# Attention of a hybrid decoder layer: head pairs packed in 32 rows and row halves, mask as bias rows, transposes moved among the projection's products

## The reference

```python
h = rmsnorm(x, g_pre1) * (1 + scale1) + shift1           # shift, scale, gate from silu(c) @ w_ada
q, k, v, f, u, bg, cg, ga, gb = split(h @ w_in)
logf = log_sigmoid(f + b_f); cum = cumsum(logf)
# prompt: 256 queries, causal.  sample: 256 cached keys (2 pages) and 4 new ones per sequence
logit[t, s] = q_t . k_s / 8 + cum[t] - cum[s]            # s <= t, else -inf
o = softmax(logit) @ v
y = bg * conv3_causal(cg * u)
m = (sigmoid(ga) * (o @ w_oa) + sigmoid(gb) * (y @ w_ob)) @ w_o
x = x + gate1 * rmsnorm(m, g_post1)
x = x + gate2 * rmsnorm(swiglu(rmsnorm(x, g_pre2) * (1 + scale2) + shift2), g_post2)
```

## Time and profile before

| | us |
|---|---|
| median of 3 runs | 1874.73 (1874.23 to 1874.82) |
| profiled execution, its own time | 1877.05 |
| its span | 1875.4 |
| TensorE busy | 1831.7 |
| DVE busy | 901.9 |
| ACT busy | 730.7 |
| POOL busy | 52.5 |

### The profile page before, as it was taken

One profiled execution on the slowest core, in us unless ns is written; L12 is line 12 of the kernel. 1 busy time (PEld: TensorE's weight loads), 2 busy tenths in 40 slices (PEclk: granted clock), 3 DMA queues, 4 the chain that ended last, 5 costly groups with the idle time before them and its releaser, 6 DMA issues.

```text
span 1875.4 us, 33218 instructions
## 1 busy us (share of the span) xinstructions
PE 1831.7 (98%) x13960; PEld 1701.7 (91%) x13960; DVE 901.9 (48%) x1102; ACT 730.7 (39%) x886; POOL 52.5 (3%) x109
## 2 busy tenths in 40 slices
PE   8999999998889999999999999999999999999997
PEld 5889988885569999999978999999999999999996
DVE  4456653326753444445457343443444445565565
ACT  3433233325653433334346333333333334445453
POOL 0001000004200000000000000000000000000000
PEclk9999999999989999999999999999999999999999
DMA  9996968874454554547875574455445445445441
GB/s 347 386 322 226 330 226 315 314 257 152 164 171 160 170 165 157 168 167 269 291 280 178 193 247 158 157 162 173 157 162 172 158 160 174 159 159 175 161 158 51
DMA packets 189562, 382.17 MB, mean 204 GB/s; under 512 B 8773, under 2 KB 9245, under 8 KB 189183
## 3 DMA queue, kind: packets, MB, share of 16 engines
q1 hardware_dynamic: 185744, 378.04, 58.3%
q0 software_dynamic: 1312, 2.58, 0.4%
q10 hardware_dynamic: 2424, 0.37, 0.1%
HBM read 376.15 MB, written 4.81 MB: 203 GB/s over the span
## 4 chain that ended last, share of the span: by engine, by line
PE 93%; DVE 2%; ACT 2%; issue 1%; DMA 1%; POOL 0%; ACTq 0%; DVEq 0%; POOLq 0%
PE bank L553 28%; PE bank L555 27%; PE bank L554 27%; PE bank L563 4%; PE bank L872 1%; PE bank L587 1%; PE bank L806 1%; PE bank L789 1%; DMA ada<-in_w_ada 1%; PE bank L571 1%; PE bank L820 0%; PE bank L824 0%; PE bank L615 0%; ACT w_hi L996 0%; DVE w_lo L1407 0%
## 5 line engine op out<-in xcount | busy, mean ns | idle before, releaser
L553 PE MATMUL bank<-a_lo,w_hi 128*128 128x288 f32 x3648 | 1084.2, 297 | 5.1 <-DVE a_lo L1555 3.2
L554 PE MATMUL bank<-a_hi,w_hi 128*128 128x288 f32 x3648 | 1076.2, 295 | 0.0
L555 PE MATMUL bank<-a_hi,w_lo 128*128 128x288 f32 x3648 | 1072.8, 294 | 0.0
L1407 DVE TENSOR_TENSOR w_lo<-raw,w_hi 128x2048 fp32r<-128x2048 f32 x244 | 559.3, 2292 | 740.3 <-ACT w_hi L996 739.5
L996 ACT CAST w_hi<-raw 128x2048 fp32r<-128x2048 f32 x244 | 465.6, 1908 | 828.0 <-PE bank L555 828.0
L553 PEld LDWEIGHTS bank<-a_lo,w_hi 128*128 128x128 f32 x3648 | 683.7, 187 | 23.7 <-issue 17.3
L555 PEld LDWEIGHTS bank<-a_hi,w_lo 128*128 128x128 f32 x3648 | 687.1, 188 | 0.0
L554 PEld LDWEIGHTS bank<-a_hi,w_hi 128*128 128x128 f32 x3648 | 685.0, 188 | 0.0
L1519 DVE TENSOR_TENSOR a_lo<-hid,a_hi 128x1152 fp32r<-128x1152 f32 x44 | 59.4, 1352 | 12.3 <-ACT a_hi L1026 12.3
L563 PE MATMUL bank<-ada,cT 128*32 128x512 f32 x544 | 63.1, 596 | 1.7 <-DMA ada<-in_w_ada 1.7
L1026 ACT CAST a_hi<-hid 128x1152 fp32r<-128x1152 f32 x44 | 50.7, 1155 | 0.0
(11 more groups left out here) (306 smaller groups left out, 1068.9 us busy)
## 6 DMA issues: line engine op xcount, KB each, us to landing
raw<-in_w_ffn_in SPq DMA_DIRECT2D x88, 1024.0 KB, 5.0
raw<-in_w_in SPq DMA_DIRECT2D x80, 1024.0 KB, 6.5
ada<-in_w_ada SPq DMA_DIRECT2D x68, 1024.0 KB, 9.1
raw<-in_w_ffn_out SPq DMA_DIRECT2D x44, 1024.0 KB, 5.1
ada_o<-in_w_ada SPq DMA_DIRECT2D x26, 1024.0 KB, 9.6
raw<-in_w_o SPq DMA_DIRECT2D x16, 1024.0 KB, 5.6
raw<-in_cache_k SPq DMA_DIRECT2D x16, 512.0 KB, 4.7
raw<-in_cache_v SPq DMA_DIRECT2D x16, 512.0 KB, 4.5
```

The lines of the kernel that those rows point to most:

```text
L553: pe.matmul(acc, w_hi[buf][:, a, cols], lo[:, kt, :], start=first and a == 0, stop=False)
L554: pe.matmul(acc, w_hi[buf][:, a, cols], hi[:, kt, :], start=False, stop=False)
L555: mm = pe.matmul(acc, w_lo[buf][:, a, cols], hi[:, kt, :], start=False, stop=last and a == SK - 1)
L1407: tt(w_lo[buf][:, :, :], raw[s][:, :, :], w_hi[buf][:, :, :].bitcast(F32), ALU.subtract).then_inc(raw_turn, 1)
```

## The change

1. **Sampled sequences.** Two head pairs share the 32 rows of a column tile (8 rows each, `q_bd` 80 wide), so that all 16 heads lie in one bank: one pass of bias rows and two passes of q by K, and P by V with 256 columns. The mask is in the bias rows (`cumk`, `selq`, prepared once by POOL); ACT takes the exponential straight from the bank.
2. **Prompt.** q is scaled when it is copied to `qT`, and `qT`, `kT` and v rows are used in place. The two heads of a pair lie on partitions 0 to 63 and 64 to 127 and are multiplied as two row tiles into banks 0 and 1; -cum (`ncum`) is added by a matmul with K = 16. The row term cum[t] is dropped, since it cancels in the softmax. P by V of the pair is issued head by head in column halves. `extra_rows`, `copy_k`, `copy_q`, `v_st` are gone.
3. **Order.** The q, k, v stage is written out: w_ada groups after products 0, 2, 5, 7, 10, 12, 15, 17; z, lf, the sums, the suffix sums, k rows, v rows 0 to 1 of the first half and the first sequence's K pages among the products. Turns 1 to 7 start with `sample_scores`. The first mix product has the last sequence's P by V inside it, `keep_warm` is gone, and the split of y follows mix product 4.

The core of the diff:

```diff
-    ADA_EVERY = 3
+    ADA_AT = (0, 2, 5, 7, 10, 12, 15, 17)
...
-                for hf in range(2):
-                    for q4 in range(4):
-                        acc = bank[6 + hf][32 * q4:32 * q4 + 32, 0:PAST + TS]
-                        pe.matmul(acc, q_bd[:, 4 * hf + q4, :], KTs[j][:, 4 * hf + q4, :], start=True, stop=False,
-                                  tile_position=(0, 32 * q4))
-                    for q4 in range(4):
-                        acc = bank[6 + hf][32 * q4:32 * q4 + 32, 0:PAST + TS]
-                        mm = pe.matmul(acc, selq[:, 4 * hf + q4, :], cumk_s[:, :], start=False, stop=True,
-                                       tile_position=(0, 32 * q4))
+                for c in range(CT):
+                    pe.matmul(bank[6][32 * c:32 * c + 32, 0:KEYS], selq[:, c, :], cumk[:, s, :], start=True, stop=False,
+                              tile_position=(0, 32 * c))
+                for r in range(2):
+                    for c in range(CT):
+                        mm = pe.matmul(bank[6][32 * c:32 * c + 32, 0:KEYS], q_bd[:, c, 32 * r:32 * r + 32],
+                                       KTs[j][:, 2 * c + r, :], start=False, stop=r == 1, tile_position=(0, 32 * c))
...
-                pe.matmul(bank[j][:, 0:P], q_st[j][:, 0:P], k_st[j][:, 0:P], start=True, stop=True)
-                pe.matmul(bank[j][:, P:3 * P], q_st[j][:, P:TP], k_st[j][:, :], start=True, stop=True,
+                for j in range(2):
+                    r0 = DH * j
+                    pick = ident[r0:r0 + H, r0 + 2 * s + j:r0 + 2 * s + j + 1].broadcast_to([H, P])
+                    pe.matmul(bank[j][:, 0:3 * P], pick, ncum[r0:r0 + H, :], start=True, stop=False,
+                              tile_position=(r0, 0), skip_group_check=True)
+                for j in range(2):
+                    rows = slice(DH * j, DH * j + DH)
+                    pe.matmul(bank[j][:, 0:P], qT[rows, s, 0:P], kT[rows, s, 0:P], start=False, stop=True,
+                              tile_position=(DH * j, 0), skip_group_check=True)
+                for j in range(2):
+                    rows = slice(DH * j, DH * j + DH)
+                    pe.matmul(bank[j][:, P:3 * P], qT[rows, s, P:TP], kT[rows, s, 0:TP], start=False, stop=True,
+                              tile_position=(DH * j, 0), skip_group_check=True).then_inc(S_ps, 1)
...
+            for u in range(QKV):
+                t = u % PER_HALF
+                product(N_QKV + u, t % 4 == 0, t % 4 == 3, G_QKV + u // 4, SK * (t % 4), a_hi, a_lo, u % SPLIT,
+                        None, first_rows if u == QKV - 1 else None)
+                if u in ADA_AT:
+                    ada_group(A_QKV + ADA_AT.index(u))
+                if u - 1 in ADA_AT:
+                    ada_transpose(A_QKV + ADA_AT.index(u - 1))
+                if u == 0:
+                    turn_z()
+                if u == 1:
+                    turn_lf()
...
+            for s in range(1, SB):
+                sample_scores(s)
+                scores(s + 1)
+                sample_values(s - 1)
+                turn_p(s, 0)
+                if s + 1 < SB:
+                    turn_k(s + 1, (0, 1))
+                turn_p(s, 1)
+                turn_o(s - 1)
+                if s + 1 < SB:
+                    turn_k(s + 1, (2, 3))
+                pair_out(s)
+                turn_s(s)
```

More of the change, by code:

```diff
@@ L716, in _ @@
[L716 to L733, removed]
@@ L854, in pair_and_sequence @@
[L854 to L873 removed]
+                if s > 0:
+                    pe.wait_ge(sP_out, s)
@@ L874, in pair_and_sequence, with turn_o @@
                 mm.then_inc(page_used, 1)
+            def turn_o(s):
+                if s < 0:
+                    return
                 pe.wait_ge(sO_sb, s + 1)
-                for hf in range(2):
-                    mm = pe.transpose(bank[5][:, hf * P:hf * P + P], o_s[:, hf, :], ident[:, :])
-                mm.then_inc(sOT, 1)
-            turn_k(0, 0, (0, 1, 2, 3))
-            scores(0, 0)
-            scores(1, 1)
-            sample_scores(0, 0)
-            with pe.Fori(0, PAGE_TURNS - 1) as i:
-                for j in range(2):
-                    pair_and_sequence(i, j, True)
@@ new lines, in pair_hi, with sample_hi @@
+            def pair_hi(s):
+                act.wait_ge(O_ps, s + 1)
+                if s == 0:
+                    act.wait_ge(s_kout, 32)
+                nc.scalar.copy(o_hi[:, s, 0:TP], bank[3][:, 0:TP]).then_inc(O_hi, 1)
+            def sample_hi(s):
+                if s < 0:
+                    return
+                act.wait_ge(sOT, s + 1)
+                for e in range(2):
+                    rows, src = sample_out(e)
+                    ins = nc.scalar.copy(sample_cols(o_hi, rows, s), src)
+                ins.then_inc(sO_hi, 1)
@@ new lines, in _ @@
+            exp_head(0, 0)
+            copy_row(act, nc.scalar.copy, 8)
+            copy_row(act, nc.scalar.copy, 10)
+            exp_head(0, 1)
+            exp_sample(0)
+            act.wait_ge(rowT_ps, len(ROWS))
+            new_keys(1)
+            copy_KT(1, 0)
+            copy_pT(0, 0)
+            copy_pT(0, 1)
+            copy_KT(1, 2)
+            exp_head(1, 0)
+            pair_hi(0)
+            for s in range(1, SB):
+                copy_pT_s(s - 1)
+                exp_head(s, 1)
+                exp_sample(s)
+                copy_o_s(s - 1)
+                copy_pT(s, 0)
+                copy_KT(s + 1, 0)
+                if s == SB - 1:
+                    act.wait_ge(s_out, 16 * 6)
+                    act.wait_ge(sS_ps, SB - 1)
+                    act.wait_ge(O_ps, SB // 2)
+                    split_hi(N_MIX, 0, R_MIX + 1, 0)
+                copy_pT(s, 1)
+                sample_hi(s - 1)
+                copy_KT(s + 1, 2)
+                exp_head(s + 1, 0)
+                pair_hi(s)
@@ L1250, in split_m @@
+            copy_pT_s(SB - 1)
+            copy_o_s(SB - 1)
             def split_m(c):
@@ L1752, in max_head, with copy_z, copy_lf @@
-            def max_head(h, j):
-                dve.wait_ge(S_ps, h + 1)
-                own.step()
+            def copy_z():
+                dve.wait_ge(z_ps, 1)
+                own.mark(nc.vector.tensor_copy(z_rows[:, 0:512], bank[6][0:2 + 2 * SB, :]))
+                nc.vector.tensor_copy(z_rows[:, 512:DC], bank[7][0:2 + 2 * SB, :]).then_inc(z_out, 1)
+            def copy_lf():
+                dve.wait_ge(lfr_ps, 1)
+                for b in range(3):
+                    rows = min(P, NT - b * P)
+                    ins = nc.vector.tensor_copy(lfr[0:rows, b, :], bank[6][0:rows, H * b:H * b + H])
+                ins.then_inc(lfr_done, 1)
@@ L1844, in mix_turn @@
                     split_lo(n + 1, (t + 1) % RAW, (t + 1) % SPLIT)
+                    if first and t == 0:
+                        sample_lo(SB - 1)
+                    if first and t == 4:
+                        for c in range(2):
+                            split_act_lo(H_HI + c, yT, SK * c, y_hi, y_lo, SK * c)
                     if t == 5:
```

1006 lines of the change are left out of this document (506 added, 500 removed).

## The result

The changed kernel takes 1840.70 us (median of 4 runs, 1839.89 to 1842.01) against 1874.78 before (median of 4 runs): 34.1 us less, a ratio of 0.9818 (95% interval 0.9801 to 0.9835). The forecast was 28.6 less, 1846.1. Two further measurements of the same kernel, made as a base for the experiments, gave 1842.11 and 1841.22, that is 33.0 and 33.7 less than the kernel before on the same chips.

What follows compares the result with a forecast made beforehand. TensorE, busy 98% of the span, was taken as the bound. Between the q/k/v and mix stages, 10.6 + 2.0 + 11.4 + 62.7 + 10.2 + 1.9 + 1.5 = 100.3 against 128.9: 28.6 us less, 1846.1; range 1838 to 1860.

Steps and rivals of the forecast that it cites:

- Moving the sums and transposes among the products: q/k/v stage: 10.6 us of TensorE work moved, still paid; the two holes there, 2.21 and 2.90 us, go.
- The new wait for copy_z: q/k/v stage: turn_lf waits on z_out while DVE has copy_z behind add_ada; 2.0 us that nothing can cover.
- The last turn: Last turn before the mix stage: slots, then a chain through w_hi, sample_hi, sample_lo and w_lo to the product; 10.2 us.
- Scores: Prompt scores of a head pair as row halves: 1.7 us taken, between 1.5 fully side by side and 2.9 in sequence.
- Half clock in the first mix product: First mix product: a clock drop expected after the last turn's two waits, costing 1.5 us.
- The w_ada groups in 18 slots: q/k/v stage: groups in 18 slots instead of 24, DMA share from 0.78 to 0.90; priced at zero.
- the turn: Middle turn of the loop: slots of 9.2 us plus three hand-over waits, 10.45 against 12.9; six turns 62.7.
- The wait for copy_o_s: Each turn, ahead of turn_k: copy_o_s must free bank 5, with turn_p's 0.35 over it; 0.45 us.
- Rival (a): Prompt scores: row halves run one after the other, 1.2 us more a pair, 8 pairs, 1856 us; chance 0.13.
- (b): Loop of turns: the clock falls once in a turn, 1.2 to 1.7 us each, 7 turns, 1856 us; chance 0.12.
- (c): Loop of turns: clock stays at half throughout, a turn 17 us, 1892 in all; chance 0.06 including another slowdown.
- Rival (d): q/k/v stage: transfers of the ada groups bind, 1850 us; counted inside the main case's chance of 0.65.

## Why the prediction was right, and where it was off

**Direction, place and main terms held.** The whole difference lies between the first q/k/v product and the first o product, as forecast. Moving the sums and transposes among the products was costed as 5.1 of holes closed and no work saved; the run that puts most of them back gets 5.1 of waits back. The new wait for copy_z was costed 2.0 and is 1.68. The last turn was 10.2 and took 9.65 through the chain that was named.

**Some agreement is luck.** Scores were put at 1.7 between bounds of 1.5 and 2.9, and took 1.70, but not by the reckoning given. In the kernel before, 256 columns take 0.43 between neighbours of the same kind (443.08 to 443.51), so 768 take 1.29, and 0.4 of the 1.70 are something else, perhaps the changes of tiling treated below. Half clock in the first mix product was costed 1.5; in the three traces of the changed kernel it is 1.3, 1.5 and 4.2 (29.0, 29.2 and 31.8, less 27.6). Half clock behind the wait for z_rows, 1.5 in two of these three, was not in the sum at all.

The w_ada groups in 18 slots cost nothing: TensorE has no wait for them in the stage.

**The step that was mis-sized is the turn**, 10.45 forecast, 9.36 measured, six times: 6.5 of the 8.9 by which the sum exceeded this execution (the forecast is 5.4 above the median). The prediction's sentence "turn_k's second half needs both copies of the first" is wrong. Page 2 goes to the bank of page 0, which ACT begins to copy while page 1 is still being turned, and turn_s needs only ACT's copy. The copies of pages 0 and 1 in the first of the six turns:

```profile
452.25 0.58 ACT L1212 COPY KTs<-bank 128x512 f32<-128x512 f32 x1 [0.25 <-PE bank L771]
452.69 0.69 DVE L1823 COPY KTs<-bank 128x512 f32<-128x512 f32 x1 [0.21 <-PE bank L771]
```

ACT's copy ends at 452.83, page 2 starts at 453.03, straight behind turn_o, and DVE's copy runs on to 453.38. So neither the 0.55 nor the 0.25 is left as a wait. With the assumed waits put in, the turn is 10.08 and the kernel 5.1 slower, so this reading is shown, not only argued. The wait for copy_o_s is 0.30, not 0.45, and the slots add up to 9.06 instead of 9.2, above all sample_scores with 1.73 for 1.87; together these are the 1.09 a turn. That sample_values came out at 1.56 is no support for the way it was costed: passes of 128 columns take only 0.08 more.

**Rival (a)**, row halves one after the other, is refuted by the traces: the same six matmuls take 1.70 in pairs and 3.38 in a row. The Trainium skill, "TensorE: Matmul & The Clock Gate", Part 3, says that matmuls in distinct row groups run concurrently; the trace agrees (1.69 for one head, 1.70 for two). Its price was too low, though: 2.9 was summed from one head's rows, where one head alone really takes 1.69. The prediction's rows for the price of a change of tiling were misread: L772 in front of L820 stands in no line of the earlier trace rows, and takes 0.52 there (505.88 to 506.40). Such changes leave no idle entry, but the slots beside them are longer: in the kernel before, 128 columns take 0.23 behind transposes (505.65 to 505.88) and 0.32 behind column tiles (504.19 to 504.51), so about 0.1 at a place. No run isolates it. The Trainium skill, "TensorEngine Tiling (Array Packing)", Key Properties, says that a switch of the tiling mode drains the array; these slots agree, with about that 0.1.

**Rivals (b) and (c)**, the clock falls in the loop, did not happen: 1.00 in all turns but the last in every trace of the changed kernel. But they were less far than the 12 and 6 in 100 suggest: with the heads apart the clock falls in four turns and ahead of the first, at 2.9 us a turn. TensorE has no gap there either, so being busy is not enough to keep the clock up; what decides it is not shown. The prediction's "3.9 us of transposes" from turn_p to pair_out is too much: a whole turn has 27 transposes, 3.1 us at 0.116. The Trainium skill, "TensorE: Matmul & The Clock Gate", Part 4, says that transposes do not count as busy in the same way; by that rule each turn would have its drop. The traces do not show that, with these 3.1 us in a turn at 1.00.

**Rival (d)**, w_ada's transfers bind, is refuted: the only wait of TensorE in that stage is for z_rows.

Of the 37.5 us between the two traces, then, 13.9 are gained up to the second sample_scores, with the moved sums and transposes (7.8 in the run that puts them back) and the shorter first turn; 21.4 in six turns (12.9 to 9.36), 5.4 in the last turn (15.1 to 9.65), and 3.2 are lost again in the first mix products (25.8 to 29.0).

## What to carry to other kernels

Cost a hand-over by the bank, not by the group: ask which copy frees the very bank that the next instruction writes, since here alternate banks and two copying engines hid all of a wait of 0.8 us a turn that a count of copies suggested. Put matmuls that use different row halves directly behind each other; the same instructions in another order cost twice and, here, the clock as well. A wait of about 2 us on the bounding engine can cost more than itself where the clock may fall behind it: taking away the wait for z_rows and shortening the chain of the last turn gave 7.3 us together, though the waits of the changed kernel add up to only 4.7.

## What the runs showed of the hardware

- The granted clock fell from 2.4 to 1.2 GHz behind a stretch with TensorE at 13.00 busy of 13.00, when each head's K=16 and K=64 matmuls ran alone in one row half; with the same matmuls in pairs it stayed up.
- The same wait of 1.7 us was followed by half clock in 7 of 11 traced executions, and not in 4; behind the hole of the last turn the half clock cost between 1.3 and 4.2 us (29.0 to 31.8 to the first o product, 27.6 without). These two account for the difference between the traces of 1839.91 and 1844.28 (1.5 and 2.9 of 4.4); whether they make the spread of the other executions is not shown.
- In the run with the row transposes behind the products, stretches with 5.1 us of holes in 10 kept full clock, where the kernel before, in the same place, fell to half.
- Rows of the array that are not used save no time: 256 columns take 0.43 to 0.52 with K=112 before, by their neighbours, and 0.53 with K=64 (446.14 to 446.67 with the heads apart). What such a matmul leaves free was won here by a neighbour in the other half.
